# Gate of the last two blocks' embeddings by seven block products instead of eight, with the projections first and the weight sums begun sooner

## What is computed

```
def finish_layer(h, att, cv, p, w_out, g_ffn, w_gate_up, w_down, g_ple, w_ple_gate, w_ple_proj):
    h = h + jnp.concatenate([att, cv], axis=-1) @ w_out
    u = rms_norm(h, g_ffn)
    gate, up = jnp.split(u @ w_gate_up, 2, axis=-1)
    h = h + (jax.nn.silu(gate) * up) @ w_down
    g = jax.nn.sigmoid(rms_norm(h, g_ple) @ w_ple_gate)
    return h + g * (p @ w_ple_proj)
```

## Time and profile before

| what | value |
|---|---|
| median of 3 runs | 2627.03 us (2625.26 to 2628.12) |
| the profiled execution's own time | 2624.12 us |
| its span, first to last instruction | 2622.3 us |
| PE busy | 2602.2 us, 14408 records |
| DVE busy | 1803.4 us |
| ACT busy | 1222.0 us |
| POOL busy | 467.1 us |
| DMA moved | 675.05 MB |

### The profile page before, as it was taken

How to read it: one execution, slowest core, us unless ns; L and a number is a source line. 1 busy time by engine, 2 the same in 40 slices (tenths; PEclk the granted TensorE clock), 3 DMA queues, 4 the chain that set the end, 5 groups by cost and what they waited for, 6 DMA issues and landing times.

```text
span 2622.3 us, 40458 instructions
## 1 busy us (share of the span) xinstructions
PE 2602.2 (99%) x14408; PEld 2542.2 (97%) x14408; DVE 1803.4 (69%) x3303; ACT 1222.0 (47%) x2240; POOL 467.1 (18%) x513
## 2 busy tenths in 40 slices
PE   9999999999999999999999999999999999999999
PEld 8999999999999999999999999999998999999999
DVE  4555478988978878777756876888548655665462
ACT  5444367877764323443334443323435443443453
POOL 6222200000001323223323323333300000000000
PEclk9999999999999999999999999999999999999999
DMA  5666798888677998898888898889895554555677
GB/s 202 213 219 233 252 356 272 266 279 267 205 236 245 296 305 281 294 345 291 319 310 313 283 322 302 318 312 317 299 317 165 169 169 153 174 162 167 196 240 236
DMA packets 316115, 675.05 MB, mean 257 GB/s; under 512 B 36589, under 2 KB 172653, under 8 KB 315373
## 3 DMA queue, kind: packets, MB, share of 16 engines
q1 hardware_dynamic: 297676, 609.55, 70.0%
q0 software_dynamic: 18240, 62.93, 6.8%
HBM read 514.28 MB, written 160.10 MB: 257 GB/s over the span
## 4 chain that ended last, share of the span: by engine, by line
PE 86%; DVE 7%; DMA 4%; issue 2%; ACT 2%; SPq 0%; DVEq 0%; ACTq 0%
PE psum L198 53%; PE psum L2285 23%; PE psum L1509 3%; PE psum L1485 2%; DMA x<-in_w_gu 2%; DVE y L2878 1%; PE psum L1473 1%; PE psum L1472 1%; DVE wres L2831 1%; ACT wres L2708 1%; DMA o_y<-c_top 0%; DVE wres L2087 0%; DVE plain L2078 0%; DMA a_cr<-in_cache 0%; PE psum L837 0%
## 5 line engine op out<-in xcount | busy, mean ns | idle before, releaser
L198 PE MATMUL psum<-uh,wres 128*128 128x416 f32 x3936 | 1118.2, 355 | 5.7 <-DVE wres L2831 2.4
L198 PEld LDWEIGHTS psum<-uh,wres 128*128 128x128 f32 x3936 | 736.6, 188 | 19.2 <-DVE wres L2831 5.3
L198 PE MATMUL psum<-ul,wres 128*128 128x416 f32 x1968 | 687.7, 349 | 0.0
L2708 ACT ACTIVATE wres<-x 128x1024 fp32r<-128x1024 f32 (+2 forms) x234 | 268.5, 1148 | 641.2 <-PE psum L198 533.1
L198 PE MATMUL psum<-wres 128*128 128x416 f32 x2304 | 447.7, 352 | 1.9 <-DVE wres L2831 1.6
L198 PEld LDWEIGHTS psum<-wres 128*128 128x128 f32 x2304 | 430.3, 188 | 9.3 <-issue 2.4
L2285 PE MATMUL psum<-wres 128*128 128x416 f32 x2056 | 418.7, 352 | 4.3 <-issue 1.4
L2285 PEld LDWEIGHTS psum<-wres 128*128 128x128 f32 x2056 | 383.2, 188 | 13.8 <-issue 5.6
L198 PEld LDWEIGHTS psum<-ul,wres 128*128 128x128 f32 x1968 | 370.3, 188 | 6.5 <-issue 1.4
L2878 DVE SCALAR_TENSOR_TENSOR y<-c_top,vec,y 128x416 f32<-128x416 f32 (+1 forms) x600 | 340.2, 634 | 0.8
L1651 ACT ACTIVATE wres<-c_top 128x512 fp32r<-128x512 f32 (+1 forms) x306 | 184.0, 603 | 190.1 <-PE psum L2285 48.2
(11 more groups left out here) (277 smaller groups left out, 3448.5 us busy)
## 6 DMA issues: line engine op xcount, KB each, us to landing
x<-in_w_gu SPq DMA_DIRECT2D x132, 512.0 KB, 5.4
wres<-w_gu_lo SPq DMA_DIRECT2D x88, 512.0 KB, 6.2
x<-in_w_down SPq DMA_DIRECT2D x48, 704.0 KB, 5.9
w_gu_sums<-c_top POOLq DMA_DIRECT2D x60, 512.0 KB, 6.0
c_top<-w_gu_sums SPq DMA_DIRECT2D x120, 256.0 KB, 3.0
w_gu_lo<-wres SPq DMA_DIRECT2D x44, 512.0 KB, 6.5
c_top<-in_w_gu POOLq DMA_DIRECT2D x88, 256.0 KB, 5.9
wres<-w_down_lo SPq DMA_DIRECT2D x32, 704.0 KB, 7.0
```

What stands on the lines that cost most here:

```text
L198: mm = nc.tensor.matmul(out, w[wp](kw), u[up](ku), start=first and n == 0 and j == 0, stop=last and n == len(kts) - 1 and j == 2)
L2708: nc.scalar.activation(whi[v % 2][:, 0:kts, :], raw[v % 2][:, 0:kts, :], ACT.Copy).then_inc(hi_done, 1)
```

## The change

The gate of the pair is no longer 32 pieces G but 28 products "Q" (P1 to P7, four tiles each), in the order P1 0 to 3, then all sixteen projections E, then P2 0 to 3, then the list `CLOSING`. The results of the projections are copied by ACT from PSUM banks 6 and 7 to sixteen places (`proj`). The sums of right-hand sides are made by the new `last_sums(x)`, where x counts pieces from the first Q, between x = 2 and 16; ACT rounds them at x = 3, 4, 8, 9, 10 and 13. The norm of the second block is multiplied right after P1 0 and no longer after the second G. Eight rounds of weight sums are added for the gate's weights, 68 in all, and they begin at U0 + 2. ACT waits for their end at i = 12 and no longer at the pair's start. In the opening and at the end of B, ACT multiplies the upper tiles of h by the gain alone (new operations with `ACT.Identity`), DVE takes the difference to the lower tiles before the norm is known, and multiplies it by the inverse afterwards (`times`). The raw and split places of p, and the gate's `u` of the first block, lie elsewhere. The built program holds 14306 matmuls in place of 14354, 204 transfers issued by POOL in place of 180, and 1704 by SP in place of 1728.

```diff
+CLOSING = ("P6 0", "P6 1", "P5 0", "P7 0", "P5 1", "P4 0", "P3 0", "P7 1", "P6 2", "P3 1", "P4 1", "P5 2", "P7 2", "P6 3",
+           "P4 2", "P5 3", "P7 3", "P3 2", "P4 3", "P3 3")
...
+    def gate(d, p):
+        return {"op": "Q", "m": p, "d": d, "kts": KH, "summed": d in SUMMED}
...
-    for e in range(2):
-        for m in range(KD):
-            us += [{"op": "G", "e": e, "m": m, "h": h, "kts": KH, "summed": False} for h in range(2)]
-            us.append({"op": "E", "e": e, "m": m, "kts": KP, "summed": False})
+    us += [gate("P1", p) for p in range(KH)]
+    us += [{"op": "E", "e": e, "m": m, "kts": KP, "summed": False} for e in range(2) for m in range(KD)]
+    us += [gate("P2", p) for p in range(KH)] + [gate(e[:2], int(e[3:])) for e in CLOSING]
...
-SUMS = 2 * KF + 4 * CHUNKS
+SUMS = 2 * KF + 4 * CHUNKS + KD
...
+                elif n >= 2 * KF + 4 * CHUNKS:
+                    r = 2 * ((n - 2 * KF - 4 * CHUNKS) // 2) + x
+                    src = t["w_ple"][r * P:(r + 1) * P, 0:2 * KH * P].rearrange("p (h n) -> p h n", h=2)[:, :, cols]
...
-        act.wait_ge(f["sums_moved"], sums_stored(SUMS - 1))
...
+            if i == 12:
+                act.wait_ge(f["sums_moved"], sums_stored(SUMS - 1))
...
-            if 3 <= i <= 6:
-                high("t2", i - 3, "t2", t2h[i - 3], t2r[i - 3])
+            if i in (3, 4):
+                for k in (2 * i - 6, 2 * i - 5):
+                    high("t2", k, "t2", t2h[k], t2r[k])
...
+                if m >= KH:
+                    nc.scalar.activation(b22r[m - KH], hb[:, m, :], ACT.Identity,
+                                         scale=vec[:, V_GFFN + m:V_GFFN + m + 1]).then_inc(u_hi, 1)
...
+                if op == "B" and m >= KH:
+                    nc.scalar.activation(b22r[m - KH], hb[:, m, :], ACT.Identity,
+                                         scale=vec[:, V_GPLE + m:V_GPLE + m + 1]).then_inc(u_hi, 1)
...
+            if op == "B" and (m, u["c"]) == (2, 4):
+                p_high(0)
...
+            if op == "B" and (m, u["c"]) == (6, 4):
                 p_high(1)
...
+            if x == 1:
+                root(3, 5, sb)
+            if x in (3, 4):
+                for k in (2 * x - 6, 2 * x - 5):
+                    high("qt2", k, "qt2", t2h[k], t2r[k])
+            if x == 8:
+                for k in K4:
+                    high("qt3", k, "qt1", t3h[k], t3r[k])
+            if x == 9:
+                for k in K4:
+                    high("qt1", k, "qt1", t1h[k], t1r[k])
+            if x == 10:
+                for k in K4:
+                    high("qt4", k, "qt4", t4h[k], t4r[k])
+            if x == 13:
+                for k in K4:
+                    high("qb22", k, "qub4", b22h[k], b22r[k])
...
             if op == "E":
+                copy(proj[u["e"] * KD + m], bank(6 + m % 2), e_out)
...
+            if op == "Q" and u["d"] in ("P1", "P6", "P5"):
+                act.wait_ge(used, U + n + 1)
+                if (u["d"], m) == ("P1", 0):
                     act.wait_ge(hid_lo, F0 + split_at[0, KF - 1])
-                for cols in HALVES if n == NP - 2 else [slice(0, N)]:
-                    nc.scalar.activation(sig(m)[:, cols], bank((u["e"] * KD + m) % 3)[:, cols], ACT.Sigmoid).then_inc(sig_out, 1)
+                if (u["d"], m) == ("P1", 2):
+                    act.wait_ge(p_lo, SINGLE + 2)
+                copy(q_tile[u["d"]][m], bank(m), kept)
+            if op == "Q" and u["d"] in ("P2", "P7", "P4"):
+                act.wait_ge(left, L0 + left_at["q", u["d"], m])
+                nc.scalar.activation(q_tile[u["d"]][m], q_tile[u["d"]][m], ACT.Sigmoid).then_inc(sig_out, 1)
+            if op == "Q" and u["d"] == "P3":
+                act.wait_ge(used, U + n + 1)
+                for cols in HALVES if n == NP - 1 else [slice(0, N)]:
...
+        def finished(d, p):
+            e, m = output(d, p)
+            o, v, h = done_at[d, p] - 1, q_tile[d][p], hb if e else ha
+            for i, cols in enumerate(HALVES if o == 2 * KD - 1 else [slice(0, N)]):
+                dve.wait_ge(sig_out, S0 + sig_at["q", d, p, i])
+                dve.wait_ge(e_out, YB + e * KD + m + 1)
+                nc.vector.tensor_tensor(v[:, cols], v[:, cols], proj[e * KD + m][:, cols], ALU.mult).then_inc(gs_out, 1)
+                dve.wait_ge(gs_out, G0 + KF + o + 1 + i)
+                nc.vector.tensor_tensor(v[:, cols], v[:, cols], h[:, m, cols], ALU.add).then_inc(y_out, 1)
 
...
-            if 2 <= i <= 5:
-                k = i - 2
-                scaled(b12r[k], hb, k, V_GFFN, sb, 1)
-                scaled(b22r[k], hb, k + KH, V_GFFN, sb, 1)
-                less(t3r[k], b12r[k], b22r[k], ("ub4", k))
-                less(t2r[k], uar[k], t3r[k], ("t3", k))
-            if 3 <= i <= 6:
...
+            if i in (2, 3):
+                dve.wait_ge(n_r, NN + 2)
+                for k in (2 * i - 4, 2 * i - 3):
+                    times(t3r[k], ("gap", k))
+                    less(t2r[k], uar[k], t3r[k], ("t3", k))
+            if i in (3, 4):
+                for k in (2 * i - 6, 2 * i - 5):
+                    u_low("t2", k, t2l[k], t2r[k], t2h[k])
+            if i in (4, 5):
+                for k in (2 * i - 8, 2 * i - 7):
+                    scaled(b12r[k], hb, k, V_GFFN, sb, 1)
...
+            if i == 10:
+                for k in K4:
+                    times(b22r[k], ("gap", k))
...
+        def last_sums(x):
+            def times(dst, need):
+                dve.wait_ge(u_raw, raw_at[need])
+                nc.vector.tensor_tensor(dst, dst, sb, ALU.mult).then_inc(u_raw, 1)
+            if x in (2, 3):
+                dve.wait_ge(n_r, NN + 4)
+                for k in (2 * x - 4, 2 * x - 3):
+                    times(t3r[k], ("qgap", k))
+                    less(t2r[k], uar[k], t3r[k], ("qt3", k))
+            if x in (3, 4):
+                for k in (2 * x - 6, 2 * x - 5):
+                    u_low("qt2", k, t2l[k], t2r[k], t2h[k])
+            if x in (5, 6):
+                for k in (2 * x - 10, 2 * x - 9):
+                    scaled(b12r[k], hb, k, V_GPLE, sb, 3)
+            if x == 7:
+                for k in K4:
+                    less(t1r[k], b12r[k], uar[k], ("qub", k))
+            if x == 8:
+                for k in K4:
+                    dve.wait_ge(made, MT + KH + k + 1)
+                    dve.wait_ge(u_raw, raw_at["qt3", k])
+                    nc.vector.tensor_tensor(t4r[k], dr[k], t3r[k], ALU.add).then_inc(u_raw, 1)
+            if x == 12:
+                for k in K4:
+                    times(b22r[k], ("qgap", k))
+            for e, name, low, src, hi in ((9, "qt3", t3l, t3r, t3h), (10, "qt1", t1l, t1r, t1h), (14, "qb22", b22l, b22r, b22h),
+                                          (16, "qt4", t4l, t4r, t4h)):
+                if x == e:
...
+        pool.wait_ge(u_lo, T0 + lo_at["pa", KD - 1])
         for k in K4:
             nc.gpsimd.tensor_tensor(dr[k], uar[KH + k], uar[k], ALU.subtract).then_inc(made, 1)
...
+            elif op == "Q":
+                d = u["d"]
+                if d == "P1":
+                    if m == 3:
+                        pe.wait_ge(n_sd, NN + 3)
                     else:
-                        b_, m_ = divmod(e * KD + m - 3, KD)
-                        pe.wait_ge(sig_out, S0 + sig_at["g", b_, m_, 0])
-                name = "pb" if e else "pa"
-                rights = (PB if e else UA)[h * KH:(h + 1) * KH]
-                mm = product(bank((e * KD + m) % 3), w, rights, h == 0, h == 1,
-                             (lambda k: pe.wait_ge(u_lo, T0 + lo_at[name, h * KH + k])) if m == 0 else None)
+                        evicted(*(("gb", KF - 2), ("gb", KF - 1), ("ga", KF - 1))[m])
+                elif d == "P2":
+                    if m == 1:
+                        pe.wait_ge(n_sd, NN + 4)
+                    else:
+                        evicted(*(("B", 4), None, ("q", "P2", 0), ("q", "P2", 1))[m])
+                elif d == "P7":
+                    evicted("q", *(("P2", m + 2) if m < 2 else ("P4", m - 2)))
+                elif d == "P4":
+                    evicted("q", "P7", m)
+                else:
+                    pe.wait_ge(kept, KEPT + kept_at["q", {"P6": "P1", "P5": "P6", "P3": "P5"}[d], m])
+                ready = {"P1": lows("pa"), "P2": lambda k: lows("pa")(k + KH), "P6": lows("qt2"), "P5": lows("qt1"), "P7": lows("qt3"),
+                         "P4": lows("qt4"), "P3": lows("qb22")}[d]
+                mm = product(bank(4 + m % 2 if d in ("P2", "P7", "P4") else m), w, RIGHT[d], d in ("P1", "P2", "P7"), True,
+                             None if m else ready, d not in ("P1", "P2", "P7"))
             else:
...
-                if e == 0 and m < 4:
-                    evicted("B", m + 4)
+                if e == 0 and m < 2:
+                    evicted("B", m + 6)
                 else:
-                    pe.wait_ge(e_out, unit(e, m) - 3)
+                    pe.wait_ge(e_out, YB + e * KD + m - 1)
```

(9 more changed lines are left out.)

200 lines of the change are left out of this document (115 added, 85 removed).

## The result

The changed kernel took 2644.67 us (median of 5, 2642.71 to 2648.2) beside 2627.03 for the kernel before: ratio 1.0069, 95% interval 1.0058 to 1.008. That is 17.6 us slower; I had said 6, and a range up to 2644.

The account below looks back on a forecast made before the run. PE, busy 99% of the span, was taken to bound the kernel. Terms summed to +6.2 us on the profiled 2624.1, giving 2630.3, and 2.9 for the median made 2633 us, range 2621 to 2644.

Parts of the forecast that it names:

- Matmuls, -9.1: In the gate, 48 fewer matmuls at 0.189 us each, all on the path: -9.1 us.
- Opening, -2: Pair's opening: fewer DVE operations ahead of P6 0 remove its 0.93 us stall, later stalls remain: -2 us.
- The norm's wait, +4.4: Closing: PE waits 5.1 us in place of 0.7 before the norm's matmul: +4.4 us, bounds +2.4 and +5.1.
- The clock: Rival for the closing: PE's clock falls to 1.2 GHz after the norm's stall, +6.8 us, 2640 us; chance 10%.
- Projections, +6.4: Closing's sixteen projections: ACT's bunched roundings and copies, with two banks, stall PE: +6.4 us, between 0 and 8.
- Rest of the closing, +2: Closing: added DVE operations and a last product with sigmoid and two operations behind it: +2 us, 0 to 5.
- Weight sums, +4.5: POOL's rounds share DMA engines and slow DVE: +3 us early, +1.5 us late from 1900 to 1940 us.
- the five signs that I named: Changed profile: norm idle about 5 us, ACT stalls 1.4, over 134 opening matmuls, early transfers over 6.5 us, clock at 9s.
- Neither condition under which I said the forecast fails: P1 0 to last projection under 32 us, or pair beginning over 10 or under 1 us later than before.
- Rival B: DMA costs: early chain pays both transfers fully, +6, late stretch overfills its engines, +5; 2640 us, chance 20%.

Follow-up runs that it names:

- e9: Changed kernel without the eight added rounds of sums, the other 60 begun at U0 + 16, leaving the gate's numbers wrong; 2632.75 us.
- e13: Kernel before with the changed kernel's 68 rounds of sums, begun after the second unit, and ACT's wait for their end; 2639.0 us, ratio 1.0039.
- e12: Changed kernel with e9's sums, the norm two products later, four PSUM banks for the projections, and roundings spread over pieces 10 to 22; 2629.36 us.
- e16: Changed kernel with e14's closing and e9's sums, so the gate's numbers are wrong; 2625.33 us, ratio 0.9985.
- e1: Changed kernel with 24 idle matmuls put on PE after P1 0, ahead of the norm's matmul in the closing; 2645.2 us.
- e3: Changed kernel with the projections written to four PSUM banks in turn in place of two; 2644.39 us.
- e7: Changed kernel with the closing's norm two products later, four PSUM banks for projections, and t4's and b22's roundings moved to pieces 20 and 22; 2640.72 us.
- e10: Changed kernel with the closing's norm two products later, four PSUM banks, and roundings laid one or two a piece over pieces 10 to 22; 2641.86 us.
- e14: Changed kernel, norm two products later, four PSUM banks, ACT's roundings placed where DVE has made their operands, DVE's t1 and t4 sums before low halves; 2640.47 us.
- e4: Kernel before with its 60 rounds of weight sums begun after the second unit in place of the sixteenth; 2632.36 us, ratio 1.0023.
- e6: Changed kernel with 64 rounds of sums from U0 + 16 on and four after the pair's last hidden tile; 2636.35 us.
- e5: Changed kernel with 60 rounds of sums from U0 + 16 on and eight after the pair's last hidden tile; 2649.26 us.
- e15: Changed kernel with e14's closing, sums begun after the ninth unit and the last two rounds behind POOL's differences; 2636.4 us, ratio 1.0029.

## Why the prediction was wrong

The direction held, the size did not: +17.6 measured, +6.2 summed. By its own steps:

- **Matmuls, -9.1.** Right: the 48 are gone.
- **Opening, -2.** Half of it. Between kernels that differ in the opening alone, P1 0 to P6 0 is 19.1 us (e9) for 19.9 (before), and 20.0 on average of seven changed kernels with the full sums for 20.8 (e13). Counted on to the 300th matmul from P1 0 it is nearly all of it: 61.0 us on average of e9, e12 and e16 for 62.8. The stall of 0.93 is gone, the later ones stayed as I said. The 134 matmuls that I started from count those across the edges of three windows twice; one window of 30 us has 130.
- **The norm's wait, +4.4.** Measured 5.75 - 0.69 = +5.1, my upper bound. The last square's sum, 0.59 us in the earlier trace rows, took 1.50 beside POOL's differences. I had priced POOL at 0.2 us in all.
- **The clock.** This step failed: the sum had nothing for it, the rival had 10%, and it came. It cost 3 us, not 6.8, since the clock was back after some 6 us; e1 shows that these matmuls were slow by the clock. It does not show that a filled hole saves the loss, for there the same 3.4 us went in the projections.
- **Projections, +6.4.** Measured +5.3 (23.5 for 18.1), of which 4.1 in four stalls released by ACT's copies, as foreseen. The mechanism that I gave was only its surface: banks (e3, 22.7 us), order (e7, 24.3, of which 1.7 are the clock) and spreading (e10, 23.9) changed it little. ACT's list asks for sums that DVE, which works for some 22 us from the reciprocal on with at most one gap of 1 us, has not made. e14 shows it (19.7), though it moves ACT's roundings and DVE's low halves at once.
- **Rest of the closing, +2.** What is left, 1.8 us for P2 and the first two P6 and 0.7 behind them, is of that size.
- **Weight sums, +4.5.** This is the step that failed most. Measured 11.9 (e9) and 11.6 (e13), 13 and 10 by the ratios. Two things were missed. (1) Early, I priced two transfers; the rounds meet the whole stretch from 768 to 900 us. The first O is at 1946.6 to 1954.9 in seven profiles with the late start, mean 1949.9, and at 1955.0 to 1961.9 in nine with the early one, mean 1958.4: 8.5 us where I took 3 and bounded at 7 (e4, the early start alone: 4.8 by the medians, 6.5 in its profile). (2) Late, I looked at 1900 to 1940 us, which did stay full, and took the end at 1973 for safe by 30 us because I asked only who *waits* for the sums. The last store was issued at 1991 in the changed kernel, and the rounds share the DMA engines with O's weights: 37.5 us from O to P1 0 in the runs with 60 rounds, 40.0 with 68, and up to 2.4 more at the opening's norm. PE waits for `w_out_lo` in ten of the twelve profiles with 64 or 68 rounds (0.4 to 1.7 us) and in none of the six with 60; in e7, where the last store was issued at 1948.5, ahead of the first O, O to P1 0 is 37.8 us and neither wait is there.

With these the sum is -9.1 - 0.9 + 5.1 + 3 + 5.3 + 2.5 + 11.9 = +17.8, for +17.6 by the medians.

Of the five signs that I named, the norm's idle, the transfers over 6.5 us and stalls of the projection run by ACT came. Those stalls were 0.9 to 1.2 us, not 1.4. The count of matmuls came too, 142 in the 30 us from P1 0 on, but the kernel before has the same 142 there, so it could tell nothing. The clock did not stay at 9s in the windows that matter, though the page's 40 slices still show 9s: a slice is 66 us wide and hides a dip of 5. Neither condition under which I said the forecast fails was met (42.1 us from P1 0 to the last projection, 7.9 us at the pair's start), so they were set too wide. Rival B named DMA with +11, and the measured price of the sums was 12, but it was given 20% and had neither the clock nor the last rounds beside O in it.

What stays open: what the eight rounds cost by themselves, and why so much. Between kernels that differ in the sums the medians give 4 us (e6 less e9, interval some 4 to either side) to 17 (e5 less e9), and 11 to 15 with the closings of e10, e14 and e15 (less e12 and e16). Placed in the pair's last pieces they stalled PE on weight transfers (e6). No run separates what POOL's transfers cost from what its additions cost DVE: the early stalls are released by DVE's low halves, behind longer transfers and beside POOL's operations.

## What to carry to other kernels

Price background transfers by the work that shares the engines with them, not by who waits for their end; and test them alone, on the unchanged kernel (one number, e4), before building on them. Where an in-order engine serves two others, place each of its instructions by when its operand is *made*: spreading a bunch evenly won nothing as long as each still stood ahead of its operand. When an operation is pulled forward to shorten a chain, ask what PE does until it can run; filling the hole here only moved the fall of the clock to the next stalls.
